# Expert stage of a mixture-of-experts layer: turning, copying and splitting the next block's gathered rows between the two k halves of a block

## The reference

```python
def expert_block(xs):
    tok, g, e = xs
    xb = x_pad[tok]
    hb = jax.nn.silu(xb @ w_exp_gate[e]) * (xb @ w_exp_up[e])
    return (hb @ w_exp_down[e]) * g[:, None]
```

## Time and profile before

| | |
|---|---|
| median of three runs | 2318.41 us (2318.08 to 2320.51) |
| the profiled execution's own time | 2317.46 us |
| its span, first to last instruction | 2315.7 us |
| busy share: TensorE, VectorE, ScalarE, GpSimd | 81%, 57%, 44%, 27% |
| mean granted clock of TensorE | 0.896 |
| expert stage in the span | from the first load at 779.19 us to about 1426 us |

### The profile page before, as it was taken

How to read it: one execution, slowest core, us unless ns; L and a number is a source line. 1 busy time by engine, 2 the same in 40 slices (tenths; PEclk the granted TensorE clock), 3 DMA queues, 4 the chain that set the end, 5 groups by cost and what they waited for, 6 DMA issues and landing times. The chain is left out here.

```text
span 2315.7 us, 28502 instructions
## 1 busy us (share of the span) xinstructions
PE 1872.5 (81%) x8582; PEld 1457.1 (63%) x8582; DVE 1309.8 (57%) x1609; ACT 1014.8 (44%) x1304; POOL 633.3 (27%) x422
## 2 busy tenths in 40 slices
PE   5790489999482399999999995068989886998999
PEld 2770257777362288888888884056666555887887
DVE  1625234444546399999999993736555664323332
ACT  1211044442210288888888883125455543223221
POOL 0698700000001356666666662001111110000000
PEclk9795689999785599999999997579989998999999
DMA  6541532212200599999999993543221002332321
GB/s 235 178 168 62 147 103 75 66 55 78 95 20 1 193 355 362 380 358 373 374 368 368 348 364 110 228 98 84 53 58 42 19 10 82 96 103 71 105 96 73
DMA packets 167638, 373.65 MB, mean 161 GB/s; under 512 B 39820, under 2 KB 77224, under 8 KB 159112
## 3 DMA queue, kind: packets, MB, share of 16 engines
q1 hardware_dynamic: 148888, 325.58, 41.0%
q0 software_dynamic: 18672, 47.05, 5.9%
HBM read 355.90 MB, written 29.29 MB: 166 GB/s over the span
## 5 line engine op out<-in xcount | busy, mean ns | idle before, releaser
L108 DVE TENSOR_TENSOR exp_parts<-exp_raw,exp_parts 128x2048 fp32r<-128x2048 f32 x192 | 435.0, 2291 | 56.4 <-ACT exp_parts L1677 55.9
L1677 ACT CAST exp_parts<-exp_raw 128x2048 fp32r<-128x2048 f32 x192 | 365.1, 1915 | 93.5 <-DMA exp_raw<-in_w_exp_up 80.2
L102 PE MATMUL ps<-exp_parts,xgT 128*128 128x512 f32 x1536 | 377.7, 401 | 6.6 <-issue 6.3
L102 PEld LDWEIGHTS ps<-exp_parts,xgT 128*128 128x128 f32 x1536 | 286.6, 190 | 77.1 <-issue 11.9
L102 PE MATMUL ps<-exp_parts,exp_hT 128*128 128x512 f32 x768 | 196.4, 405 | 2.1 <-DVE exp_hT L108 2.1
L102 PE MATMUL ps<-h4T,w_up_parts 128*128 128x512 f32 x768 | 175.7, 392 | 8.6 <-ACT w_up_parts L144 8.6
L102 PE MATMUL ps<-w_down_parts,hidden_parts 128*128 128x512 f32 x768 | 176.5, 393 | 7.1 <-DVE w_down_parts L108 7.1
L1570 POOL DMA_INDIRECT xg<-h_rows,row_index x64 | 148.6, 2322 | 110.0 <-issue 106.1
L102 PEld LDWEIGHTS ps<-h4T,w_up_parts 128*128 128x128 f32 x768 | 145.2, 189 | 39.0 <-ACT w_up_parts L144 8.9
L102 PEld LDWEIGHTS ps<-w_down_parts,hidden_parts 128*128 128x128 f32 x768 | 145.7, 190 | 37.9 <-issue 7.5
L102 PE MATMUL ps<-h3T,w_parts 128*128 128x512 f32 (+1 forms) x576 | 156.7, 426 | 14.7 <-DVE w_parts L108 14.7
(11 more groups left out here) (424 smaller groups left out, 3166.9 us busy)
## 6 DMA issues: line engine op xcount, KB each, us to landing
exp_raw<-in_w_exp_gate SPq DMA_DIRECT2D x130, 512.0 KB, 6.1
exp_raw<-in_w_exp_up SPq DMA_DIRECT2D x130, 512.0 KB, 8.0
exp_raw<-in_w_exp_down SPq DMA_DIRECT2D x64, 1024.0 KB, 7.9
w_up_raw<-in_w_up SPq DMA_DIRECT2D x15, 1024.0 KB, 5.2
w_down_raw<-in_w_down SPq DMA_DIRECT2D x15, 1024.0 KB, 5.1
yk<-y_rows SPq DMA_DIRECT2D x8, 1536.0 KB, 16.9
w_raw<-in_w_in SPq DMA_DIRECT2D x42, 256.0 KB, 3.4
modw_first<-in_w_mod POOLq DMA_DIRECT2D x9, 1024.0 KB
```

The source lines that it names most:

```text
L102: mm = nc.tensor.matmul(out, left[a], right[b], start=start and i == 0, stop=stop and i == 2)
L108: return nc.vector.tensor_tensor(dst, x, high.bitcast(F32), ALU.subtract)
L1677: nc.scalar.copy(dst, src).then_inc(s_hi[kind], 1)
```

## The change

TensorE turns the rows of block b+1 between the first and the second half of gate/up of block b, instead of behind both. ScalarE copies them out of PSUM between high A(b+1) and high B(b+1), instead of behind the sigmoid. VectorE splits them between low A(b+1) and low B(b+1), instead of behind the products of h. No instruction is added, removed or resized; the semaphores and their values are the same.

```diff
@@ step, TensorE
                 gate_up(b, u, 0)
-                gate_up(b, u, 1)
                 if more:
                     turn_rows(b + 1, u + 1, i, False)
+                gate_up(b, u, 1)
                 if not (first and u == 0):
                     down(b, u, first)
                 pe.wait_ge(s_h, b + 1)
@@ step, ScalarE
                 if more:
                     high(A, b + 1, u + 1, first, i)
+                    high_rows(b + 1, u + 1)
                     high(B, b + 1, u + 1, first, i)
                 act.wait_ge(s_piece, done(B, b, first, u))
                 if not start:
                     act.wait_ge(s_g, b)
                 nc.scalar.activation(sg[:], g.ps[:, 2 + u % 2, 0:F], ACT.Sigmoid).then_inc(s_sg, 1)
-                if more:
-                    high_rows(b + 1, u + 1)
                 high(C, b, u, first, i)
@@ step, VectorE
                 if more:
                     low(A, b + 1, u + 1, first)
+                    low_rows(b + 1, u + 1)
                     low(B, b + 1, u + 1, first)
                 bank = g.ps[:, 2 + u % 2, :]
                 dve.wait_ge(s_sg, b + 1)
@@
                 nc.vector.tensor_tensor(h[:], bank[:, F:2 * F], h[:], ALU.mult).then_inc(s_h, 1)
-                if more:
-                    low_rows(b + 1, u + 1)
                 low(C, b, u, first)
```

## The result

The changed kernel takes 2404.12 us (median of four runs, 2398.69 to 2410.44) against 2318.35 us: a ratio of 1.0369, 95% interval 1.0342 to 1.0396. It is slower by 86 us, twice the 43 us that were forecast, and outside the range of 2337 to 2378. Its profiled execution took 2405.95 us with a span of 2404.2 us.

A forecast was written before the change was run, and what follows sets the result against it. It took TensorE's 9.50 us step, a 9.64 us ScalarE-VectorE chain and the loop end as bounds. Steps of 10.29 us gave 644.9 - 602.5 + 1 = +43.4 us on 2317.46: 2361 us, range 2337 to 2378.

The forecast's parts named there:

- The wait on h: TensorE, end of each expert-stage step: the transposes of h wait about 0.8 us for the second product of h.
- The eight terms up to the load for h's transposes: Delays from a step's first matmul through turn, rows' copy, high B, low B and products of h, reaching 9.92 us.
- What the change takes away: Low of the rows leaves the step's end; its 13.60 us chain goes; otherwise steps would fall to 9.50 us plus loop end.
- the last term: TensorE, step's end: 0.37 us from the load for h's transposes to the next block's first matmul, making 10.29 us a step.
- the forecast's sum: 62 steps of 10.29 us plus 6.9 for loop ends, 644.9 against 602.5, plus 1 for the first step: +43.4 us.
- the loop's end: TensorE's branch, once in four steps: 0.46 us taken whole, 15 times, 6.9 us in all.
- cover of 1.03 us: Before the change, the second product of h was done 1.03 us before TensorE came for it; now 1.76 us later.
- SyncE: Weight-load queue: raw weights B come free about 1.6 us later in the step; cost taken as zero.
- GpSimd: Gather queue: gathers wait for a turn 2.83 us earlier, wanted equally earlier; 5 us left over two steps, price zero.
- the rival: GpSimd's copies and gathers fall back, the turn of rows waits for its gather, loops of 11.0 us: 2398 us; 8%.
- the joint holds: High B, low B or products run 0.8 us sooner, h ready at 9.1, TensorE's 9.50 us step rules: 2311 us; 7%.
- half of it: About half the waiting on h occurs, joints 0.35 us shorter, 9.94 us a step: 2338 us; 8%.

## Why the prediction was wrong

**The wait on h: right.** The eight terms up to the load for h's transposes held to 0.03 us each and 0.03 in the sum. The load for h waits 0.86 us; the forecast said about 0.8.

**What the change takes away: right.** No gate/up load waits for low of the rows any more, and the run with the products ahead of low B reaches steps of 9.51 us, the forecast's 9.50.

**The step that failed is the last term**, "load for h's transposes to the next block's first matmul: 0.37". It was read from a step of the kernel before in which h was done 1.03 us ahead of the array, so that TensorE's sequencer was through its conditions by the time the array got to h, and carried into a step in which the array waits for h. It measured 0.98. The conditions, register steps and waits are in no list of busy work, and behind a wait for the step's last operand they come one after another. The run without conditions, at 10.27 a step and 2361 us, is what the forecast's sum stood for: it is the changed kernel without the term that I left out. From block 0's load for h to block 62's it takes 646.1 us, against 644.9 in the sum, though its first step alone was 12.84. That its median and the forecast agree to 1 us is partly luck; its profiled execution took 2367.62. The forecast did see this for the loop's end ("the branch stands behind the waiting transposes, so I take its 0.46 us whole"; measured 0.51) and did not ask the same of the conditions in every step.

The same failure sits in the forecast's cover of 1.03 us. Within the loop, the next block's matmul comes no sooner than 1.02 us behind h in any step of the kernel before, of the changed kernel or of the run with the products ahead of low B; in the kernel before, in the step of the rows, it came 1.40 us behind. So h could become 0.38 us later for nothing, not 1.03. It came 1.79 us later (9.89 into the step instead of 8.10), and 9.50 + 1.79 - 0.38 = 10.91 is the step that was measured, 10.93. The loop's end is the same path: 1.54 us from h to the next matmul in the changed kernel, 1.50 in the kernel before (h done at 1376.98, matmul at 1378.48).

**The account.** From block 0's load for h to block 62's, 685.8 us were measured where the sum said 644.9. Of the 40.9 us between, the 58 steps of the loop carry 0.66 each on average, 38; the one step of 13.21 us carries 2 more; the first step, 11.46 instead of 10.29, one. That last one is not the term that failed: its first 12 matmuls took 4.19 us instead of 3.04, and in the kernel before, too, the first step's 24 took 7.39 where later ones take 5.85. The sum had taken all 62 steps as ordinary ones. Outside these 62 steps, the load for h of block 0 stands 4.6 us later than before, 3.0 of them because the first turn of the profiled execution came at 791.70 instead of 788.68, ahead of which nothing was changed; the rest is the longer first step, for which 1 us had been allowed. Behind them, the step from block 62 to block 63, taken as unchanged, takes 9.52 us instead of 8.63, because block 62's h is late as well.

**SyncE: right.** ScalarE waits for weights only at the stage's start in the changed kernel. In the run with the products ahead of low B it does wait for them, in half of the steps.

**GpSimd: right, though the number points to the rival.** That rival named 2398 us, close to what was measured, and its mechanism did not occur. The turn of rows waited for a gather only at the stage's start, and GpSimd now waits for y in each step:

```profile
L1577 POOL COPY out_index<-row_asg_cols x64: 185/1380/1411, 820.4 to 1512.1; 128x1 uint32 x64
its engine sat idle before it (us, times) until:
  ACT exp_y L1689: 75.5, 64
```

Its copy even became shorter, 1.38 us in the median against 2.27 before. A number that fits is no sign for its cause.

**The other rivals** (the joint holds, 2311; half of it, 2338) did not occur: the joints up to the load for h held.

## What to carry to other kernels

What stands behind a wait in an engine's program (conditions, register steps, further waits, the loop's branch) is hidden only while the engine still has earlier work to do; once the engine is idle at that wait, it is paid in full. So when a change delays the operand of a wait on the engine that sets the time, measure the cover not up to the waiting instruction but up to the next one behind the bookkeeping (here 0.38 us, not 1.03), and ask of each joint taken from the old trace whether the sequencer was already through there. And before a copy is moved ahead of another on an in-order engine, look for who is queued two engines further on: here the order copy, high B, low B, products of h made h late, and moving two short products past one long subtraction gave it back.

## What the runs showed of the hardware that was not expected

- In the kernel before, the compare behind the wait for h ran 1.0 us ahead of the array's load for h (1386.6 and 1387.61), as soon as h was done. Three compares and a register step, with the next block's waits, take some 0.95 us from the first compare to the next block's first matmul (1206.6 to 1207.56) when they are not hidden.
- A satisfied wait is not free there: six more cost 0.33 us a step behind the wait for h.
- Removing all conditions took 0.66 us from an ordinary step of one kernel (10.93 to 10.27) and nothing that can be told from the other (2318.64 to 2316.94 us, interval 0.9980 to 1.0002).
- The one step of 13.21 us, and the nine in the run with more waits, in which 12 gate/up matmuls took 1.5 us longer at the top of the loop, are not explained. The rows show no operand that came late. Transfers of code do not explain those of the running stage: between 900 and 1500 us of the run with more waits, where eight of the nine lie, the profile has no packet in an instruction queue. Nor is it only the top of the loop: the run with the products ahead of low B has one such group of 4.29 us at 1171.88, inside an iteration.
